# One sequence beside the gathered rows, two attention units in flight, routing in parts of 2, 2 and 4 heads

## The reference

```python
mod = silu(c) @ w_ada + b_ada                      # six vectors of 2048 per sequence: w_ada is 2048 x 12288
h   = rms_norm(x, g_norm1) * (1 + scale) + shift
z   = h @ w_in                                     # q (16 heads x 64), three k/v pairs, gates, pooling input u
o   = attention(compressed, selected, window) + causal pooling of u
x1  = x + gate1 * (concat(o) @ w_out)
h2  = rms_norm(x1, g_norm2) * (1 + scale2) + shift2
# expert retrieval: 8 heads, product keys, 16 experts per head and token
q   = (h2 @ peer_wq).reshape(T, 8, 2, 128)
s   = einsum('thpd,phkd->thpk', q, peer_subkeys)   # 2 x 128 scores per head
s1, i1 = top_k(s[:, :, 0], 16); s2, i2 = top_k(s[:, :, 1], 16)
sc, j  = top_k(s1[..., :, None] + s2[..., None, :], 16)     # 16 of 256 sums
eid = i1 * 128 + i2 (at j);  g = softmax(sc)
a   = gelu(einsum('td,thkd->thk', h2, peer_u[eid]))
y   = x1 + gate2 * einsum('thk,thkd->td', g * a, peer_v[eid])
```

## Time and profile before

| | before |
|---|---|
| median of 3 runs | 2500.57 us (2497.73 to 2501.94) |
| the profiled execution | 2505.45 us, span 2503.6 us |
| DVE busy | 1756.9 us (70%) |
| PE busy | 1272.2 us (51%) |
| POOL busy | 1182.3 us (47%) |
| bytes moved by DMA | 944.54 MB, mean 377 GB/s |

### The profile page before, as it was taken

How to read it: one execution, slowest core, us unless ns; L and a number is a source line. 1 busy time by engine, 2 the same in 40 slices (tenths; PEclk the granted TensorE clock), 3 DMA queues, 4 the chain that set the end, 5 groups by cost and what they waited for, 6 DMA issues and landing times.

```text
span 2503.6 us, 18678 instructions
## 1 busy us (share of the span) xinstructions
PE 1272.2 (51%) x6783; PEld 704.6 (28%) x6785; DVE 1756.9 (70%) x2243; ACT 214.4 (9%) x559; POOL 1182.3 (47%) x686
## 2 busy tenths in 40 slices
PE   5799989893862552567959950000035556100000
PEld 3343434751321432454425920000012222000000
DVE  1010021148779978996759659999999997999898
ACT  3110032000010221211001010000000000000000
POOL 1000000002346644664325217688877676787784
PEclk9899979897885665556986965555567766655555
DMA  9979999659999989999998979999999999999897
GB/s 312 378 309 422 397 370 230 244 183 422 385 402 382 409 349 394 412 410 364 419 421 310 416 298 422 356 412 421 421 414 410 414 411 414 422 422 422 369 422 301
DMA packets 150533, 944.54 MB, mean 377 GB/s; under 512 B 18027, under 2 KB 31923, under 8 KB 44318
## 3 DMA queue, kind: packets, MB, share of 16 engines
q0 software_dynamic: 94784, 682.66, 66.9%
q1 hardware_dynamic: 55663, 260.74, 28.4%
HBM read 937.36 MB, written 10.26 MB: 378 GB/s over the span
## 4 chain that ended last, share of the span: by engine, by line
PE 28%; DMA 23%; DVE 23%; POOL 15%; issue 9%; ACT 1%; SPq 1%; POOLq 0%; DVEq 0%; ACTq 0%
POOL arena L662 11%; DMA arena<-in_peer_u,arena 10%; DVE arena L1966 8%; DMA arena<-in_peer_v,arena 6%; POOL arena L674 4%; DVE arena L1989 4%; DMA arena<-in_w_ada 4%; PE PS L1436 3%; PE PS L1414 3%; PE PS L1459 3%; PE PS L1162 2%; PE PS L1249 2%; PE PS L961 2%; PE PS L1070 2%; DVE arena L2022 2%
## 5 line engine op out<-in xcount | busy, mean ns | idle before, releaser
L662 POOL DMA_INDIRECT arena<-in_peer_u,arena x256 | 469.4, 1833 | 439.9 <-DVE arena L1966 235.2
L1966 DVE CUSTOM_DVE_ANT_0 arena<-arena 128x2048 f32<-128x2048 f32 x256 | 580.9, 2289 | 110.8 <-DMA arena<-in_peer_u,arena 109.6
L1989 DVE SCALAR_TENSOR_TENSOR arena<-arena 128x2048 f32<-128x2048 f32 x226 | 531.1, 2350 | 108.3 <-DMA arena<-in_peer_v,arena 103.1
L662 POOL DMA_INDIRECT arena<-in_peer_v,arena x256 | 428.8, 1675 | 351.0 <-DVE arena L1989 224.0
L1459 PE MATMUL PS<-arena 128*128 128x512 f32 x240 | 175.8, 901 | 450.7 <-DMA arena<-in_peer_v,arena 450.7
L1459 PEld LDWEIGHTS PS<-arena 128*128 128x128 f32 x240 | 68.2, 298 | 558.9 <-issue 551.9
L1465 PE MATMUL PS<-arena 128*64 128x512 f32 x8 | 5.4, 830 | 346.0 <-DVEq L2032 346.0
L2022 DVE SCALAR_TENSOR_TENSOR arena<-arena 128x2048 f32<-128x2048 f32 x64 | 150.6, 2352 | 10.8 <-DMA arena<-in_peer_v,arena 5.3
L961 PE MATMUL PS<-arena 128*32 128x512 f32 x768 | 119.2, 720 | 66.2 <-DMA arena<-in_w_ada 62.9
L2019 DVE CUSTOM_DVE_ANT_0 arena<-arena 128x2048 f32<-128x2048 f32 x64 | 144.9, 2291 | 8.1 <-DMA arena<-in_peer_u,arena 6.4
L674 POOL DMA_INDIRECT arena<-in_peer_v,arena x64 | 126.5, 1977 | 39.0 <-issue 18.6
(11 more groups left out here) (341 smaller groups left out, 1858.8 us busy)
## 6 DMA issues: line engine op xcount, KB each, us to landing
arena<-in_w_ada SPq DMA_DIRECT2D x96, 1024.0 KB, 13.0
arena<-in_w_in SPq DMA_DIRECT2D x32, 1048.0 KB, 10.0
arena<-in_peer_wq SPq DMA_DIRECT2D x32, 1024.0 KB, 10.3
arena<-in_w_in SPq DMA_DIRECT2D x32, 768.0 KB, 9.3
arena<-in_w_out SPq DMA_DIRECT2D x24, 1024.0 KB, 31.2
arena<-in_w_out SPq DMA_DIRECT2D x16, 512.0 KB, 27.2
arena<-in_peer_u,arena POOLq DMA_INDIRECT x320, 13.9
arena<-in_peer_v,arena POOLq DMA_INDIRECT x320, 15.4
```

Of the source, the lines that this page charges most:

```text
L662: pool.indirect_dma_start(out=rows_ring[:, k % NROW, :], out_offset=None, in_=tables[kind], in_offset=bass.IndirectOffsetOnAxis(ap=ids[:, ...
L1966: V.tensor_tensor_reduce(out=buf, in0=buf, in1=h2(t), scale=1.0, scalar=0.0, op0=ALU.mult, op1=ALU.add, accum_out=dots[:, t, r:r + 1]).the ...
L1989: V.scalar_tensor_tensor(out=acc[t], in0=rows_ring[:, k % NROW, :], scalar=dots[:, t, r:r + 1], in1=acc[t], op0=ALU.mult, op1=ALU.add).the ...
```

## The change

The three generators become one, `chain`, which goes on across the row phases; only before row 0 of tile 1, and before rows 32 and 64 of tiles 0 and 1, `reach` drives it on until the part of the routing that these rows need is done. Tiles 0 and 1 are routed in parts of 2, 2 and 4 heads (tile 2 as before in 4 and 4), so that `s_eid` is raised after 2 heads (32 rows). Only the first part of tile 0 is computed before the rows begin; the second stands before the q norm and the third between the q norm and the k norm.

In the prompt attention DVE runs max(8) and max(9) first, and then norm(u), a row, max(u+2), two rows. In the sample attention PE runs keys and scores of units 0 and 1 first; in iteration b it takes keys(b+2) after the transposes and scores(b+2) after the values; DVE's order is norm(b), two rows, max(b+2), two rows. On ACT `expert_exp` of the second and third part of tile 0 stand behind the copies of the second half of the input projection, and `gelu(0)` stands between the two halves of the output projection. SP loads the first two pieces of w_out after the cached values of all sample units instead of before them. The pauses differ: 24 and 24 rows ahead of the two halves of the output projection (20 and 20 before), 28 ahead of the routing of tile 1 (30 before).

```diff
-Q_PAUSE, K_PAUSE, S_PAUSE, OUT_PAUSE, WQ_PAUSE = 12, 20, 3, 20, 30
+OUT_PAUSE, WQ_PAUSE = (24, 24), 28
+PARTS = [[(0, 2), (2, 2), (4, 4)], [(0, 2), (2, 2), (4, 4)], [(0, 4), (4, 4)]]
+PARTS_BEFORE = [0, 3, 6]
 LOOP_ROW0 = N_INLINE * 128 - NROW
 SECTION = 512
 
@@ -520,7 +522,7 @@
             sp.wait_ge(s_parkx, 16)
             load(n_tile0 + 2, n_in1)
 
-            sp.wait_ge(s_eid, 2)
+            sp.wait_ge(s_eid, 3)
             sp.dma_start(biasP.rearrange("p a b -> p (a b)"), I["k_bias"]).then_inc(s_bp, 16)
             sp.dma_start(biasCS.rearrange("p a b -> p (a b)"), I["k_bias_cs"]).then_inc(s_bs, 16)
             sp.wait_ge(s_free, n_in1)
@@ -566,7 +568,6 @@
 
             sp.wait_ge(s_oc, 16)
             sp.dma_start(biasS.rearrange("p a b -> p (a b)"), I["k_bias_s"]).then_inc(s_bs, 16)
-            load(n_in1, n_in1 + 2)
             for b in range(DB):
                 if b >= 1 and b + 2 < DB:
 
@@ -575,6 +576,7 @@
 
                 wait(sp, q_o, b - 1)
                 cached(b, 1, vpage[b % 2], s_vpage[b % 2])
+            load(n_in1, n_in1 + 2)
 
             sp.wait_ge(q_oc, 2 * DB)
             sp.dma_start(X1_12[:, 0, :], I["x_prompt"][0, 128:256, :]).then_inc(s_x, 16)
-                    if kind == "u" and r % 64 == 0:
-                        pool.wait_ge(s_eid, 2 * t + r // 64 + 1)
+                    if kind == "u" and r in (0, 32, 64):
+                        pool.wait_ge(s_eid, 3 * t + r // 32 + 1)
@@ -801,18 +803,18 @@
                 act.wait_ge(s_scp, k + 1)
                 A(sc0[:, 0, 4 * k:4 * k + 4, :].rearrange("p a b -> p (a b)"), PS[:, 4 + k, :], copy).then_inc(s_sc, 1)
 
-            def expert_exp(t):
-                for half in range(2):
-                    w = gw[:, t, half * HH:(half + 1) * HH]
-                    act.wait_ge(s_e2, 2 * t + half + 1)
-                    A(w, w, exp).then_inc(s_e2x, 1)
+            def expert_exp(t, part):
+                h0, nh = PARTS[t][part]
+                w = gw[:, t, h0:h0 + nh]
+                act.wait_ge(s_e2, PARTS_BEFORE[t] + part + 1)
+                A(w, w, exp).then_inc(s_e2x, 1)
 
             def gelu(t):
                 act.wait_ge(s_dots, t + 1)
                 A(dots[:, t, 0:NROWS[t]], dots[:, t, 0:NROWS[t]], ACT.Gelu).then_inc(s_gelu, 1)
 
 
-            expert_exp(0)
+            expert_exp(0, 0)
 
             used(act, "ia", NK - 1, 1)
             for n in range(2):
@@ -830 (ScalarE, after the copies of the keys and values of tiles 1 and 2)
+            expert_exp(0, 1)
+            expert_exp(0, 2)
@@ -879
-            gelu(0)
@@ -892,21 +895,26 @@
                     v = Ps[:, b % 2, lo:hi]
                     A(v, v, exp, bias=nm[:, b % 2, k:k + 1], scale=SC_QK, accum_out=sm[:, b % 2, k:k + 1]).then_inc(q_exp, 1)
             kt_out(0)
+            kt_out(1)
             s_exps(0)
+            s_exps(1)
             for b in range(DB):
-                if b + 1 < DB:
-                    kt_out(b + 1)
-                    s_exps(b + 1)
                 act.wait_ge(q_T, b + 1)
                 A(PTs[:, b % 2, 0:512], PS[:, 6, :], copy).then_inc(q_TA, 1)
                 A(PTs[0:TS, b % 2, 512:768], PS[0:TS, 7, 0:256], copy).then_inc(q_TA, 1)
                 A(PTs[0:NS_C, b % 2, 768:896], PS[0:NS_C, 7, 256:384], copy).then_inc(q_TA, 1)
+                if b + 2 < DB:
+                    kt_out(b + 2)
                 act.wait_ge(q_o, b + 1)
                 for dup in range(2):
                     o = 128 + dup * TS + b * DT
                     A(OT12[:, 0:8, o:o + DT], PS[:, 7, 448:512].rearrange("p (a b) -> p a b", a=8), copy).then_inc(q_oc, 1)
+                if b + 2 < DB:
+                    s_exps(b + 2)
 
             for h in range(2):
+                if h == 1:
+                    gelu(0)
                 act.wait_ge(s_gp, 5 + h)
                 for k in range(2):
                     for m in range(2):
@@ -924 (ScalarE, after the scores of tiles 1 and 2)
+            for part in range(3):
+                expert_exp(1, part)
...
@@ -1370,10 +1380,9 @@
                 last.then_inc(q_S, 1)
             s_keys(0)
             s_scores(0)
+            s_keys(1)
+            s_scores(1)
             for b in range(DB):
-                if b + 1 < DB:
-                    s_keys(b + 1)
-                    s_scores(b + 1)
                 pe.wait_ge(q_pn, b + 1)
                 wait(pe, q_TA, 3 * b)
                 wait(pe, q_oc, 2 * b)
@@ -1383,6 +1392,8 @@
                 for k, at_ in enumerate((256, 576)):
                     turn(PS[0:TS, 7, k * 128:(k + 1) * 128], P[:, at_:at_ + TS], ident)
                 turn(PS[0:NS_C, 7, 256:384], P[:, 640:760], ident).then_inc(q_T, 1)
+                if b + 2 < DB:
+                    s_keys(b + 2)
                 pe.wait_ge(q_TA, 3 * b + 3)
                 pe.wait_ge(s_vpage[b % 2], N_VPAGE[b % 2] + 48 * (b // 2 + 1))
                 pt = PTs[:, b % 2, :].rearrange("p (a b) -> p a b", a=7)
@@ -1395,6 +1406,8 @@
                         for odd in range(2):
                             last = mm(PS[64 * odd:64 * odd + 64, 7, 448 + g * 16:464 + g * 16], lhs, rhs[:, odd], start=(i == 0), stop=(i == 6), tile_position=(0, 64 * odd))
                 last.then_inc(q_o, 1)
+                if b + 2 < DB:
+                    s_scores(b + 2)
             pe.wait_ge(q_oc, 2 * DB)
 
 
@@ -1415,7 +1428,7 @@
                     last.then_inc(s_free, 1)
                 pe.wait_ge(s_gb, 8)
             for n in range(4):
-                pe.wait_ge(s_x1, 6)
+                pe.wait_ge(s_x1, 5 if n == 0 else 6)
                 wait(pe, s_h2, 4 + n - 1)
                 for m, chunk in enumerate((4, 3)):
                     for k in range(2):
@@ -1735
...
-            def experts(t, half):
+            def experts(t, part):
...
+                h0, nh = PARTS[t][part]
...
-                    dve.wait_ge(s_sc, 2 + 2 * half)
+                    dve.wait_ge(s_sc, (h0 + nh) // 2)
...
                 if t < 2:
                     dve.sem_inc(s_eid, 1)
+                    yield ("experts", t, part)
@@ -1838,10 +1855,9 @@
                     last = V.tensor_scalar(Ps[:, b % 2, lo:hi], Ps[:, b % 2, lo:hi], sm[:, b % 2, k:k + 1], None, ALU.mult)
                 last.then_inc(q_pn, 1)
 
-            def beside_dots():
+            def chain():
 
                 yield from experts(0, 1)
-                yield from pause(Q_PAUSE)
                 V.memset(qkr[:, 2, :], float(HD))
                 dve.wait_ge(s_z1, 5)
                 for t in (1, 2):
@@ -1853,10 +1869,9 @@
                 link(V.reciprocal(qkr[:, 1:3, 0:NH], qkr[:, 1:3, 0:NH]))
                 for t in (1, 2):
                     link(scale_by_rms(t, 0))
-                    yield
                     scale_by_gain(t, 0)
                     yield
-                yield from pause(K_PAUSE)
+                yield from experts(0, 2)
                 dve.wait_ge(s_z1, 9)
                 for t in (1, 2):
                     for k in (1, 2):
@@ -1880,7 +1895,7 @@
                 link(V.tensor_scalar(GK[0:TS, 2, :], GK[0:TS, 2, :], 1.0, None, ALU.add))
                 V.reciprocal(GK[:, 1, :], GK[:, 1, :])
                 V.reciprocal(GK[0:TS, 2, :], GK[0:TS, 2, :]).then_inc(s_gk, 1)
-                yield from pause(4)
+                yield from pause(3)
                 cmp_shift(1, 6)
                 yield from pause(2)
                 for c in range(8):
@@ -1888,47 +1903,50 @@
                     V.tensor_tensor(DTt12[:, c, 0:16], PS[:, 3 + c % 3, 0:16], DX[:, c, :], ALU.add).then_inc(s_dx, 1)
                     if c % 2 == 1:
                         yield
+                yield
+                cmp_norm(1)
                 yield from pause(3)
-                cmp_norm(1)
+                p_max(8)
+                p_max(9)
+                yield
+                for u in range(8, 16):
+                    p_norm(u)
+                    yield
+                    if u + 2 < 16:
+                        p_max(u + 2)
+                        yield from pause(2)
                 yield from pause(4)
-                p_max(8)
-                for u in range(8, 16):
-                    yield
-                    yield
-                    p_norm(u)
-                    if u < 15:
-                        yield
-                        p_max(u + 1)
-                    yield
-
-            def beside_sums():
-
-                yield from pause(S_PAUSE)
                 dve.wait_ge(s_bs, 32)
                 dve.wait_ge(s_gsi, 16 * NH)
                 s_max(0)
+                s_max(1)
+                yield
                 for b in range(DB):
+                    smp_norm(b)
                     yield from pause(2)
-                    smp_norm(b)
-                    if b + 1 < DB:
+                    if b + 2 < DB:
+                        s_max(b + 2)
                         yield from pause(2)
-                        s_max(b + 1)
-                    yield from pause(2)
```

(37 more changed lines are left out.)

36 lines of the change are left out of this document (19 added, 17 removed).

## The result

The changed kernel takes **2557.8 us** (median of 4 runs, 2551.8 to 2559.5) against 2500.0 us of the kernel before on the same chip (2497.7 to 2501.9): ratio 1.0227, 95% interval 1.0208 to 1.0246. The forecast was 2527 us, a difference of +27; measured is +57.8. The sign and the waits inside both attentions were as forecast; three waits were not foreseen, the sizes fell short, and one term, the tile change, missed by 16 us.

The account below looks back on a forecast made before the run. Transfers bound it: 944.54 MB at 422 GB/s are 2238 of 2503.6 us. Terms -8.7 + 1 + 0 + 13.7 + 29 - 11.7 + 3.3 = +26.6 us on the median 2500.6 give 2527 us; range 2482 to 2558.

Parts of the forecast that it names:

- the tile change: Wait for tile 1's scores, then its routing: -11.7 us as rows and w_ada pieces fill the wait, +3.3 for routing.
- First rows: First routing of tile 0: row 0 issued 13.9 us earlier, 8.7 us gained, less 1 us for later routing beside rows.
- the third part beside the rows: Tile 0's third routing part after the projection: 11 us of VectorE lag inside 15 us of buffer credit, +1 us.
- Prompt attention: VectorE stands 2.1 us a unit for scores, stretch 106 us, 30 us unused instead of 16.3: +13.7 us.
- Sample attention: TensorE and VectorE take turns, 20.5 us a unit, stretch 143 us, 35 to 36 us unused instead of 6.8: +29 us.
- factor of 0.81 for the high level: Sample attention at TensorE's high clock: keys 1.60 us instead of 1.97, a unit 18.1 us, the term +12 us.
- K norm to the first maximum and output projection: Two stretches around the attentions: unused time as before, 10 us in the first, no difference forecast for either.
- Routing of tile 1: Stretch after the scores' wait: 171 us on VectorE against 156.6 of transfers, 14.4 unused instead of 11.1: +3.3 us.
- Slower still: Rival: both attentions at their upper price, +20 and +38 us, not given back at tile 1: 2543 us, chance 0.11.
- Faster: Rival: high clock in both attentions, tile 1 wait filled, routing covered, first rows gain 13.9 us: 2483 us, chance 0.21.
- no change: Rival: high-clock attention terms, +7 and +12 us, with the forecast's other terms, +3 in all: 2503 us, chance 0.09.
- Doesn't do what it says: Rival: chain comes late, VectorE is stopped at row 256, the 11.7 us are not gained: 2539 us, chance 0.04.

Follow-up runs that it names:

- before_parts: Kernel before the change, with only tile 0's routing in three parts and the k norm kept at its row: 2497.0 us, ratio 0.9981.
- bias_pause: Changed kernel with nine rows instead of four ahead of the first sample maximum: 2548.4 us, ratio 1.0170.
- samp_scores_first: Changed kernel with TensorE issuing the scores of sample unit b+2 ahead of the values of unit b: 2541.3 us, ratio 1.0160.
- flight_pause: flight_best with gelu(0) earlier (2500.4 us), then six more rows ahead of the compressed keys' shift and normalization, gelu another unit earlier: 2489.1 us, ratio 0.9954.
- half_rows: Changed kernel with VectorE adding only 1024 of 2048 columns of rows 196 to 255, all transfers kept: 2529.1 us, ratio 1.0110.
- pause_packed: flight_pause with the second and third routing part of tile 1 packed one step a row again: 2496.4 us, ratio 0.9979.
- tile1_paced: Changed kernel with the second and third routing part of tile 1 at one step every second row: 2545.8 us, ratio 1.0182.
- prompt_one: Changed kernel with VectorE's order in the prompt attention put back to one unit ahead, four rows a unit: 2548.5 us, ratio 1.0176.
- flight_best: Changed kernel with samp_scores_first, six rows a sample unit, bias_pause, tile1_paced, four rows a prompt unit, cache copy at row 76, gelu(0) behind unit 5's output copy: 2508.2 us.

## Why the forecast had the sign and missed the size

**First rows: right, the gain smaller.** Row 0 at 545.1 (forecast 547), TensorE's second projection half from 590.8 (591), as its timeline and VectorE's show:

```profile
545.15 2.29 DVE L1986 CUSTOM_DVE_ANT_0 arena<-arena 128x2048 f32<-128x2048 f32 x1 [6.02 <-DMA arena<-in_peer_u,arena]
...
590.79 3.70 PE L1285 MATMUL PS<-arena 128*128 128x512 f32 x8 [2.88 <-ACT arena L823]
```

The term is -4.6 instead of -7.7 us; before_parts gives -5. Cut at row 0 in both (561.1 before), 12.3 us are unused ahead of it and not 20.1, near the forecast's -8.7; from there to the k norm 8.6 are, and 5.4 before. The +1 us for the third part beside the rows was too small.

**Prompt attention: mechanism right, one wait missing.** VectorE's waits from 787 to 899 us (line, releaser, total, times, longest):

```profile
DVE arena L1844 <- DMA arena<-in_k_bias_s: 13.1, 1, 13.1
DVE arena L1659 <- PE PS L1329: 12.2, 6, 2.3
```

Six waits of 2 us on the scores, forecast 2.1 each; units 11.7 to 12.3 us apart, forecast 11 to 12.4. The transfers were right: 111.7 us at 292 GB/s are 77.3 us of them, forecast 76.6. The length was not, 111.7 us for 106 (and the summands 68, 18, 12 and 6 make 104). The sample bias was in the sum as 12 us of transfers for it and the pages, but not as a stand of 13.1 us: its issue waits for the last prompt output, and only four rows lie between. bias_pause shows that this stand costs 14 us. The term is +18.1 for +13.7.

**Sample attention: right.** VectorE and then TensorE in one unit:

```profile
937.59 0.17 DVE L1850 RECIPROCAL arena<-arena 128x3 f32<-128x3 f32 x1
...
952.41 0.49 DVE L1844 CUSTOM_DVE_ANT_0 arena<-PS,arena 128x320 f32<-128x320 f32 x1 [8.88 <-PE PS L1379]
...
958.06 0.17 DVE L1850 RECIPROCAL arena<-arena 128x3 f32<-128x3 f32 x1
...
939.16 1.12 PE L1391 MATMUL PS<-arena 128*128 128x128 f32 x4 [7.29 <-DVE arena L1855]
...
942.56 7.10 PE L1407 MATMUL PS<-arena 128*64 128x16 f32 x112
949.59 2.76 PE L1379 MATMUL PS<-arena 64*32 64x256 f32 x40
```

The reader sees two engines taking turns: TensorE idle 7.29 us for the norm, VectorE 8.88 us for the scores, the unit 20.5 us (937.59 to 958.06), as forecast. Five of the waits are of 8.88 us, the first is 6.57; the stretch 143.0 us long, forecast 143. Unused was 41.3 and not 35 to 36: 33 rows, nine page loads and the rest carried 101.7 us of transfers (143.0 x 300 / 422), not 108. With the order alone mended (samp_scores_first) the stands went from 51.0 to 15.6 us in all: the cause is shown.

The prediction weighed two levels of the clock, with a unit length for each. The granted clock was 0.51 in this stretch, which is the low level; scores and values took 2.76 and 7.10 us. In samp_scores_first they take 1.50 and 4.29 in the later unit shown, and the clock reads 0.60 over the stretch. So the factor of 0.81 for the high level, taken from key transposes between 960 and 966 us, where the clock reads only 0.74, was too near 1: with 1.50 and 4.29 a unit would take some 17 us and not 18.1 (an estimate from these rows). The Trainium skill's "TensorE: Matmul & The Clock Gate", section "HAM oscillation — how this bites in real kernels", has short bursts between waits bring the array back to its slow clock; the trace agrees, with 20.5 and not 18.1 us.

**K norm to the first maximum and output projection**: 0 forecast, -0.9 and -2.8 read. The first of them hides two new stands of VectorE, 8.0 us for the bias of the compressed keys and 6.9 for ScalarE's exp (0.8 before). They cost nothing visible here, but with the other stands gone, filling them was among what brought 11 us (flight_pause).

**Tile change: the step that failed.** VectorE's wait for the scores is 20.66 us (forecast 22.5):

```profile
1355.97 0.88 DVE L1735 MAX8 arena<-arena 128x8 f32<-128x128 f32 x4 [20.66 <-ACT arena L934]
```

and 2.9 us went unused around it, better than the 6 forecast. The term that failed is the next one, "Routing of tile 1": VectorE 171 us (49 rows and 56 us of routing), transfers 156.6, unused 14.4 and so +3.3. Measured are 33.5, +22.4. The summands were nearly right: to row 256 VectorE is busy 200.3 us with 61 rows of 2.35, which leaves 57 us for the routing. The overlap was wrong. The step set one sum against the other as if the 32 us of w_ada pieces could lie anywhere in the stretch, but they were through after 65 us. Until then the transfers were the bound, and VectorE stood 8 us for rows; from then on only rows were left, at VectorE's pace. So the routing ended after 184.8 us and not 171, with 31 us unused. And the sum ended there, while VectorE stays behind for 11 more rows (3 us more). The windows of the changed kernel, first these three and then shorter ones, show the turn:

```profile
1356.00:1421.00 65.00, 26.83 (x128) 3.21 (x128) 57.03 (x102) 1.40 (x2) 15.91 (x16) 0.54 0.98 405
1421.00:1540.80 119.80, 4.83 (x24) 1.30 (x16) 117.39 (x183) 6.28 (x12) 36.34 (x33) 0.50 0.89 323
1540.80:1567.10 26.30, 0.00 (x0) 0.00 (x0) 25.88 (x12) 0.00 (x0) 23.02 (x11) 0.50 0.97 372
...
1400.00:1420.00 20.00, 7.74 (x32) 0.81 (x32) 13.43 (x28) 0.00 (x0) 4.50 (x5) 0.50 1.01 422
...
1440.00:1460.00 20.00, 0.00 (x0) 0.00 (x0) 19.47 (x21) 0.00 (x0) 7.04 (x7) 0.50 0.95 345
...
1480.00:1500.00 20.00, 0.00 (x0) 0.00 (x0) 19.76 (x36) 0.00 (x0) 4.84 (x6) 0.50 0.87 299
1500.00:1520.00 20.00, 1.42 (x8) 0.92 (x12) 19.69 (x32) 0.74 (x2) 5.53 (x5) 0.50 0.83 295
```

With the wait's gain that is +7.6 us for the whole tile change where -8.4 was forecast: 16 of the 25 us by which the sum missed. half_rows shows that VectorE is the bound there: with less work a row the rate is 422 GB/s. pause_packed and tile1_paced put 6 to 11 us of it down to the packing, with intervals that touch those of their pairs: the old order spread its second half over every second row, which the prediction did not price.

**The rivals.** "Slower still" (2543) came nearest in time. Its attention terms, +20 and +38, lie closer to the measured +18.1 and +34.5 than the forecast's 13.7 and 29; but it left the tile change as it was, so it missed the same step. "Faster" and "no change" fell by their condition: units of 20.5 us, over 16, at the low clock. "Doesn't do what it says" fell too: row 256 follows row 255 at 1567.1 without a gap.

## What to carry to other kernels

Two units in flight pay only if each in-order queue issues what the other engine needs next ahead of what it can do later; moving one step in TensorE's queue took the stands of VectorE in the sample attention from 51 to 16 us. Where transfers bound the kernel and the consumer has 0.1 us a row to spare, sum work and transfers up to the point where the consumer has caught up, and only against those transfers that are still outstanding at that point. A chain of work that is moved by some rows meets other fixed points: the gelu that row 128 needs made VectorE stand 13 to 15 us, the bias loads 8 and 13 us, and before it stood for none of them.

## What was not expected of the hardware

The time that SyncE's queue takes to issue the same pair of page loads varies widely: 1.44 us in the changed kernel (5 us after the copy of the window cache was issued), 15.13 us in prompt_one (12 us after it), and up to 8.26 us in flight_pause, over 160 us after it. So the copy alone doesn't explain it, and the cause stays open. In prompt_one TensorE stood 11.8 us for such pages, and VectorE waited 22.1 us for the scores.

A gelu between exps costs ScalarE two table loads of 1.28 us for 0.31 us of work (flight_best, 1025.47 and 1027.10).
